# Transformer blocks in one Trainium2 kernel: new orders at the input, in the mixer and in the router, and a memory attention that writes its output by features

## The reference

```python
def causal_depthwise_conv(x, w, b): ...     # width 4, per channel
# hybrid mixer: qk = silu(conv(qk)); the gates i_pre, f_pre are 8 more columns of the same projection

def memory_cross_attention(xn, mn, w_xq, w_xkv, w_xo):
    q = (xn @ w_xq).reshape(B, S, 4, 256)
    k, v = jnp.split(mn @ w_xkv, 2, axis=-1)          # 256 memory rows, 4 heads of 256
    p = softmax(einsum('bshd,bmhd->bhsm', q, k) * 256 ** -0.5)
    return einsum('bhsm,bmhd->bshd', p, v).reshape(B, S, 1024) @ w_xo

# mixture: top group of 4, then top 2 of its 8 experts
g_logits = xt @ w_rg + b_rg;  e_logits = xt @ w_re + b_re
# each token goes to 2 experts; every expert computes (silu(xb @ w1) * (xb @ w3)) @ w2 on blocks of 128 rows
```

## Time and profile before

| | |
|---|---|
| time, median of 3 runs | 2686.95 us (2686.38 to 2688.21) |
| the profiled execution | 2689.78 us, of which its span is 2688.1 us |
| PE busy | 2583.1 us (96%) |
| DVE busy | 1519.3 us (57%) |
| ACT busy | 1238.3 us (46%) |
| POOL busy | 109.4 us (4%) |
| mean granted clock of PE | 0.977 |

### The profile page before, as it was taken

How to read it: one execution, slowest core, us unless ns; L and a number is a source line. 1 busy time by engine, 2 the same in 40 slices (tenths; PEclk the granted TensorE clock), 3 DMA queues, 4 the chain that set the end, 5 groups by cost and what they waited for, 6 DMA issues and landing times.

```text
span 2688.1 us, 30233 instructions
## 1 busy us (share of the span) xinstructions
PE 2583.1 (96%) x12036; PEld 2100.7 (78%) x12036; DVE 1519.3 (57%) x2031; ACT 1238.3 (46%) x1593; POOL 109.4 (4%) x163
## 2 busy tenths in 40 slices
PE   7999999999999999999989999989998999999995
PEld 6767888888787787888867778878877888888884
DVE  5577443343425744434366544354346788888885
ACT  3387322222436732212233333333344787777773
POOL 0111000000230000000000000000001000000001
PEclk9989999999998999999999999999999999999998
DMA  4301234334430033342322032222306999999993
GB/s 142 125 1 32 79 110 133 119 96 139 157 118 1 1 118 110 100 151 94 126 94 94 32 133 93 80 94 77 113 1 268 405 406 406 408 407 406 407 402 143
DMA packets 156901, 431.72 MB, mean 161 GB/s; under 512 B 11067, under 2 KB 80854, under 8 KB 144342
## 3 DMA queue, kind: packets, MB, share of 16 engines
q1 hardware_dynamic: 148726, 400.35, 40.2%
q10 hardware_dynamic: 4736, 16.81, 1.5%
q0 software_dynamic: 3296, 12.58, 1.3%
HBM read 382.53 MB, written 47.19 MB: 160 GB/s over the span
## 4 chain that ended last, share of the span: by engine, by line
PE 88%; DVE 5%; ACT 2%; issue 2%; DMA 1%; POOL 0%; ACTq 0%; POOLq 0%; DVEq 0%
PE ps L314 19%; PE ps L315 19%; PE ps L316 19%; PE ps L2654 6%; PE ps L2652 6%; PE ps L2653 6%; PE ps L996 2%; PE ps L2634 1%; PE ps L1934 1%; PE ps L1641 1%; PE ps L962 1%; PE ps L1614 1%; DVE area L2039 1%; PE ps L2081 1%; PE ps L2681 1%
## 5 line engine op out<-in xcount | busy, mean ns | idle before, releaser
L339 DVE TENSOR_TENSOR area<-area,area 128x2048 fp32r<-128x2048 f32 (+4 forms) x161 | 341.0, 2119 | 573.6 <-ACT area L333 573.6
L316 PE MATMUL ps<-area,area 128*128 128x512 f32 (+2 forms) x1712 | 665.0, 388 | 0.0
L333 ACT ACTIVATE area<-area 128x2048 fp32r<-128x2048 f32 (+4 forms) x161 | 284.5, 1768 | 573.9 <-PE ps L316 567.0
L315 PE MATMUL ps<-area,area 128*128 128x512 f32 (+3 forms) x1368 | 531.2, 388 | 0.0
L2625 DVE TENSOR_TENSOR area<-area,area 128x2048 fp32r<-128x2048 f32 x192 | 433.4, 2286 | 61.6 <-ACT area L2620 61.6
L314 PE MATMUL ps<-actT_parts,area 128*128 128x512 f32 (+1 forms) x984 | 390.1, 396 | 15.1 <-DVE area L339 11.5
L315 PE MATMUL ps<-actT_parts,area 128*128 128x512 f32 (+1 forms) x984 | 388.5, 395 | 0.0
L316 PEld LDWEIGHTS ps<-area,area 128*128 128x128 f32 (+1 forms) x1712 | 321.8, 188 | 71.2
L2620 ACT ACTIVATE area<-area 128x2048 fp32r<-128x2048 f32 x192 | 360.7, 1912 | 18.9 <-PE ps L2654 15.2
L315 PEld LDWEIGHTS ps<-area,area 128*128 128x128 f32 x1368 | 259.8, 190 | 52.7
L314 PE MATMUL ps<-area,area 128*128 128x512 f32 (+2 forms) x728 | 278.8, 383 | 8.3 <-DVE area L737 8.3
(11 more groups left out here) (348 smaller groups left out, 3216.3 us busy)
## 6 DMA issues: line engine op xcount, KB each, us to landing
area<-in_w SPq DMA_DIRECT2D x96, 2048.0 KB, 9.7
area<-in_w_in SPq DMA_DIRECT2D x16, 2048.0 KB, 7.9
area<-in_l_w_gate SPq DMA_DIRECT2D x22, 1024.0 KB, 5.4
area<-in_l_w_up SPq DMA_DIRECT2D x22, 1024.0 KB, 7.9
expert_inputs<-maskz SPq DMA_DIRECT2D x39, 512.0 KB, 8.6
area<-in_l_w_in SPq DMA_DIRECT2D x9, 2048.0 KB, 8.3
expert_rows<-area ACTq DMA_DIRECT2D x32, 512.0 KB, 9.2
area<-expert_inputs SPq DMA_DIRECT2D x31, 512.0 KB, 10.1
```

The costliest lines, as they stand in the source:

```text
L315: pe.matmul(dst(r), a.l, b.h, start=False, stop=False)
L316: m = pe.matmul(dst(r), a.h, b.l, start=False, stop=end)
L333: eng.activation(w.h, raw, ACT.Copy).then_inc(w_hi, 1)
L339: dve.tensor_tensor(w.l, raw, w.high_f, ALU.subtract).then_inc(w_lo, 1)
```

## The change

It has seven parts. (1) x is loaded in four DMAs of 256 features for all tokens, PE turns it chunk by chunk, and ACT copies the odd chunks. (2) In the mixer the second pieces are split ahead of the silu of their tile on ACT, and the first piece of qk2 after the taps of c = 6 instead of c = 7. (3) The memory attention uses the class of the block before it: the exponentials are divided by their sum before the transposes, the values come out by features (4 matmuls of 128x128 a unit instead of 2 of 128x256), and ACT and DVE leave them as high and low parts. Score banks are two instead of three. There is no meeting behind it and no transposing stage. (4) The sums of squares are made ahead of the last chunk of the router's product, the spreading of the root goes, and the logits are scaled after they are turned, four instructions instead of one. (5) The low parts of the first two expert pieces come later on DVE. (6) The rows of expert 0 are made by rows (8 matmuls of 128x512 with `chosen` stationary), copied by ACT and turned like the others. (7) SP loads matrix 6 behind the rows of expert 2.

```diff
+        class WideColumns(Columns):
+            tiles = 2
+            def gathered(self, h):
+                for q in range(2):
+                    yield ps[:, self.vb[h % 2][q], :], self.oT[:, 2 * h + q, :]
+            def peak(self, dve, ch, v, bank, m1):
+                ch(dve.tensor_reduce(m1, bank, AX, ALU.max))
+            def need(self, pe):
+                return lambda k: pe.wait_ge(s_ol, self.ol0 + k + 1)
+            def pe_values(self, pe, u):
...
+                    pe.wait_ge(s_pe, self.pe0 + u + 1)
+                    if i == 0 and h >= 2:
+                        pe.wait_ge(s_ol, self.ol0 + 2 * (h - 1))
...
+                    for q in range(2):
+                        for j in range(nb):
+                            m = pe.matmul(ps[:, self.vb[h % 2][q], i * P:i * P + P], self.pair_values(2 * h + q, j),
+                                          self.PT[:, u % 2, j * P:j * P + P], start=(j == 0), stop=(j == nb - 1))
...
-            gx = Groups(8, "V" * 8)
+            gx = Groups(8, "VA" * 4)
...
-                for t in range(NT):
-                    pe.wait_ge(x_at[t], 16)
-                    for k in range(KD):
...
+                def turn_x(k):
+                    pe.wait_ge(x_at[k // 2], 16)
+                    gx.wait_free(pe, k)
+                    for t in range(NT):
                         m = pe.transpose(ps[:, gx.bank(k), t * P:t * P + P], x_rows[:, t, k * P:k * P + P], ident[:, :])
...
                 for k in range(KD):
+                    if k % 2:
+                        act.wait_ge(tr, trx + k + 1)
+                        act.activation(xT[:, k, :], ps[:, gx.bank(k), :], ACT.Copy).then_inc(ea, 1)
                     norm0.chunk_act(act, k)
...
+                    if c % 4 == 1:
+                        msp.after(act, at_qk[j])
+                    if c == 6:
+                        msp.before(act, 2)
+                    if c == 7:
+                        ij.take_act(act, ifT)
+                        msp.after(act, 2)
                     act.wait_ge(midv, cv0 + c + 1)
                     act.activation(mqk[:, c, :], acc[:, c % 2, :], ACT.Silu,
                                    bias=cols2[:, CB + c:CB + c + 1]).then_inc(mida, 1)
-                    if c % 4 == 1:
-                        msp.after(act, at_qk[j])
-                    if c == 7:
-                        msp.before(act, 2)
-                        ij.take_act(act, ifT)
-                        msp.after(act, 2)
...
+                    if c == 6:
+                        msp.before(dve, 2)
                     if c == 7:
-                        msp.before(dve, 2)
                         msp.after(dve, 2)
...
-            norm, split = out_stage(orow, I["w_xo_2"][0], G_MOE)
+            xat = WideColumns(LH * NT, lambda v: NM, sc_x, None, DH, None, DH ** -0.5,
+                              buffers=(work(to, 4, 512), work(to + 2048, 2, 512)), oT=oT, first=first,
+                              score_banks=(0, 1), turn_banks=(2, 3), value_banks=((4, 5), (6, 7)),
+                              pair_values=lambda g, j: xv[:, j, g * P:g * P + P])
+            stage(lambda pe, ch: xat.pe(pe), lambda act, ch: xat.act(act), xat.dve, None, False)
+            norm, split = product_stage(oT, xat.need, first, I["w_xo_2"][0], G_MOE, row=False)
...
             def first_rows_pe(pe):
...
-                for half in range(2):
-                    for j in range(4):
-                        for t in range(NT):
-                            m = pe.matmul(ps[:, 2 + half, j * P:j * P + P],
-                                          xn[:, t, :].rearrange("p (s k) -> p k s", k=KD)[:, 4 * half + j, :],
-                                          chosen[:, t, :], start=(t == 0), stop=(t == NT - 1))
-                    m.then_inc(m_gt, 1)
+                for c in range(2):
+                    for t in range(NT):
+                        m = pe.matmul(ps[:, 2 + c, :], chosen[:, t, :], xn[:, t, c * 512:c * 512 + 512],
+                                      start=(t == 0), stop=(t == NT - 1))
+                    m.then_inc(m_fr, 1)
+                turn_rows(pe, 0)
+            def first_rows_act(act):
+                for c in range(2):
+                    act.wait_ge(m_fr, c + 1)
+                    act.activation(XR[0][:, c * 512:c * 512 + 512], ps[:, 2 + c, :], ACT.Copy).then_inc(m_fe, 1)
...
                 norm.sums_dve(dve, gt, 1)
-                split_low(dve, 0)
-                norm.wait_row(dve)
                 dve.wait_ge(mm, rw.m0 + 1)
-                dve.tensor_tensor(LT[0:NGR + NE, :], ps[0:NGR + NE, 0, :], rxb[0:NGR + NE, :], ALU.mult).then_inc(m_lt, 1)
+                dve.tensor_copy(LT[0:NGR + NE, :], ps[0:NGR + NE, 0, :]).then_inc(m_lt, 1)
...
-                split_low(dve, 1)
+                split_low(dve, 0)
...
                 dve.tensor_copy(rowu[:, :], rowi).then_inc(m_row, 1)
+                split_low(dve, 1)
...
                     for t in range(NT):
-                        sp.dma_start(x_rows[:, t, :], I["x"][0, t * P:t * P + P, :]).then_inc(x_at[t], 16)
+                        sp.dma_start(x_rows[:, :, 256 * t:256 * t + 256],
+                                     I["x"][0].rearrange("(a p) d -> p a d", p=P)[:, :, 256 * t:256 * t + 256]
+                                     ).then_inc(x_at[t], 16)
...
                 load(5, order[5][0])
-                load(6, order[6][0])
                 sp.wait_ge(m_sc, 16 * 2 * NT)
                 load_rows(1)
                 load(4, order[4][0])
                 load_rows(2)
-                for i in range(7, 3 * NE):
+                for i in range(6, 3 * NE):
```

More of the change, by code:

```diff
@@ L1173, in act @@
                         act.wait_ge(s_o, self.o0 + NT * h + NT)
-                        act.activation(self.oT.h[self.half(h), h // 2, :], self.gathered(h), ACT.Copy).then_inc(s_oh, 1)
+                        for src, d in self.gathered(h):
+                            act.activation(d.h, src, ACT.Copy).then_inc(s_oh, 1)
             def dve(self, dve, ch):
@@ L2359, in sc_x @@
                 return m
-            attention(LH * NT, lambda v: NM, sc_x, lambda u, j: xv[:, j, (u // NT) * DH:(u // NT) * DH + DH], DH,
-                      lambda h, i: orow[:, i, h * DH:h * DH + DH], DH ** -0.5)
-            norm, split = out_stage(orow, I["w_xo_2"][0], G_MOE)
+            first, to = [], 2 * PIECE * (1 - len(pieces) % 2)
+            oT = parts(A0 + 8192, A0 + 12288, KD, S)
+            xat = WideColumns(LH * NT, lambda v: NM, sc_x, None, DH, None, DH ** -0.5,
[4 more added lines that the diff above has]
+            norm, split = product_stage(oT, xat.need, first, I["w_xo_2"][0], G_MOE, row=False)
         if on(7):
@@ L2531, in router_dve @@
                 dve.wait_ge(m_lg, 1)
-                ch(dve.tensor_tensor(LG, ps[:, 1, 0:NT * (NGR + NE)].rearrange("p (t e) -> p t e", t=NT),
-                                     rbias[:, :].rearrange("p (o e) -> p o e", o=1).to_broadcast([P, NT, NGR + NE]),
-                                     ALU.add))
+                norm.wait_col(dve)
+                for t in range(NT):
+                    ch.mark(dve.scalar_tensor_tensor(out=LG[:, t, :],
+                                                     in0=ps[:, 1, t * (NGR + NE):(t + 1) * (NGR + NE)],
+                                                     scalar=rx[:, t:t + 1], in1=rbias[:, :],
+                                                     op0=ALU.mult, op1=ALU.add))
+                ch.wait()
                 G, Ee = LG[:, :, 0:NGR], LG[:, :, NGR:NGR + NE]
```

48 lines of the change are left out of this document (31 added, 17 removed).

## The result

| | before | after | ratio of the runs, 95% interval |
|---|---|---|---|
| median | 2687.78 us | 2665.06 us (2664.27 to 2678.92, 5 runs) | 0.9927 [0.9903, 0.9951] |
| the same pair once more | 2689.86 us | 2665.99 us | 0.9903 [0.9874, 0.9932] |
| PE busy, page | 2583.1 us | 2586.1 us (second profile 2568.3) | |

By the medians the kernel became 22.7 us faster (0.8%); the forecast was 28 (2659, range 2652 to 2669). The sum was 28.5 us; by the spans of two traces, the one before and the second one after, 24.4 us came, so about 4 are missing.

The account below looks back on a forecast made before the run. PE's matmuls were taken as the bound (88% of the span), so gains come from idle time, half clock or removed work: 1.3 + 9.7 + 7.0 + 10.5 = 28.5 us, median forecast 2659 us, range 2652 to 2669.

Parts of the forecast that it names:

- the last term: From the router to expert 1: router, rows and loads together give 10.5 us, ends 6 and 13.5.
- rival (a): Clock falls in the mixer gap, at the attention's start and through expert 0's rows: 20.8 us gained, 2666; chance 0.15.
- Start: Kernel start: first copy of x at 13.87 instead of 15.13, shorter chunk period; 1.3 us, ends 0 and 2.5.
- Mixer: Mixer, ahead of qk2: earlier splitting leaves PE 2.8 us idle instead of 10.02; 9.7 us, ends 7 and 10.7.
- Memory attention: Memory attention to w_xo: transposes, low-part wait and half clock go, two score banks cost some; 7.0 us, ends 4.5 and 7.6.
- Rival (e): Memory attention: units go one after the other, 7.5 us slower in all, 2694.5; decides from 3.7 us a unit; chance 0.03.
- Router: Router: earlier sums and logits turned sooner gain 2.9 us for ranks, `chosen`, positions and the scatter.
- Rows of expert 0: Ahead of expert 0: 16 rows of 512 columns instead of 64 rows; PE starts it 5.8 us earlier, ends 0.6 and 8.2.
- Rows of expert 1: Ahead of expert 1: rows land at 2073, PE wants them at 2074.1, next to no wait; first product 2079.2 instead of 2090.33.
- The rule on the shared ports: Scatter behind the router: DVE's low part holds POOL, making scatter and expert 1's rows 1.3 to 2.3 us later.
- Rival (d): Scatter behind the router: POOL is held by DVE's low part, time 2661; chance 0.10.
- Rival (c): Experts: paced by their loads after all, so the last part gives nothing; 18 us gained, 2669; chance 0.08.

Follow-up runs that it names:

- second execution: The changed kernel run again unaltered, for a base and a second profile: profiled execution 2665.44 us, median 2665.99 us.
- first execution: The first profiled execution of the changed kernel, the slowest of its runs: 2678.92 us, with PE at half clock for 58 us in the first attention.

## Why the prediction was right in its steps but one

The time lies in the range, 6 us above the forecast, and that hides the one miss in part: up to the first product of expert 1 the last term brought 5.6 us less than forecast, and the other three together 2.0 us more. That the time nearly equals rival (a)'s 2666 is luck, as (a) had the loss in the clock at other places. Of the signs that the prediction named one failed: "next to no wait" for the rows of expert 1, where 5.77 us stood.

**Start**, 1.3 forecast, 2.3 measured. The first copy came as worked out. PE's last wait for a low part ended at 23.59 before and at 21.71 in the second execution (the two lines below), and behind it PE had no gap until the sums of squares, where the shift is 2.1 us. The term was mis-sized where I let PE's own 36 matmuls take part of the gain: they took nothing of it. The low parts of the last four chunks come up to 2.4 us earlier, but PE no longer waits for them.

```profile
23.59 0.72 PE L314 MATMUL ps<-area,actT_parts 128*128 128x416 f32 x1 [0.46 <-DVE area L450]
...
21.71 0.72 PE L314 MATMUL ps<-area,actT_parts 128*128 128x416 f32 x1 [0.45 <-DVE area L450]
```

**Mixer**, 9.7 forecast, 10.0 measured, 2.81 us of idle time left for 2.8 forecast. The half clock that I left open came for 3.4 us in the first execution and not in the second, so 8.8 is seen as well; of the eight traces with this idle time of 2.8 us, three show half clock behind it. The order read from the two lists and the durations of the kernel before were enough.

**Memory attention**, 7.0 forecast, 7.7 measured: 6.1 us until the product starts, and 1.6 from the half clock that is gone behind it; none of the ten traces with the new attention shows half clock there, so it is not chance. The first wait cost what was said. Rival (e) needed a unit of 3.7 us; 34.3 us for 16 units exclude it.

**Router**, 2.9 forecast, 3.2 measured. **Rows of expert 0**, 5.8 with the router, 5.8 measured. The granted clock stood at half from about 1.5 us ahead of the first row matmul, and 5.2 to 5.4 us of the matmuls ran at half, where I had 5. Rival (a) had half clock through all of the rows and at the start of the attention; neither came, and the one in the mixer only at times.

**Rows of expert 1.** This step failed: "rows and wish meet within 1 us". PE's wish came as forecast. Before the wait it had worked 17.4 us on expert 0 (17.3). The request for the rows was missed. I had set the scatter, the two matrices and the rows end to end at 406 GB/s: 16.2 us from the first product of expert 0 to the rows. It took 22.7 us in the first execution and 23.2 us in the second. What the runs showed in place of that: the rows can't be asked for before the scatter has landed, and the matrices, issued beside it, share the DMA engines with it, packet for packet, with the larger packets. So the scatter ended behind the matrices, 17.0 us after the first product instead of 14.9 (at 375 GB/s); then 3 us passed nearly idle, and 0.5 MB took 3.8 us from its issue, so the rows came 5.7 us behind instead of 1.3. In the terms of this kernel 4.9 us came out of router, rows and loads together instead of 10.5. The gain of the faster rows of expert 0 brought this on itself: SP waits for the turned rows before it loads matrices 3 and 5. Before, it issued these loads 11.3 us behind POOL's first scatter transfer, when the last had been issued too; now it is 7.3 us, with the last three transfers still to be issued. With matrix 5 behind it the expert parts give 18.2 - 7.7 = 10.5 us up to the turn of expert 1's products (166.33 - 148.16, less the attention). That is the number of the forecast, but in a kernel whose order the forecast didn't have.

**The rule on the shared ports.** The row shows it first: the scatter transfers took 2.23, 2.88 and 1.90 us while DVE made low parts, and 1.24 at most once these were cut short. Each of the three ended 0.8 to 1.0 us behind the low part that ran beside it. The Trainium skill, page "SBUF — State Buffer", section on who interferes with whom, has a two-input DVE operation from SBUF hold up a GpSimd instruction that reads SBUF, and the trace agrees. In the same section it says that a tensor_tensor was not seen to stall a DMA that GpSimd generates; here one did, for 1.0, 1.9 and 0.9 us, so the measurement decides. Rival (d) priced it at 2 us of PE's time; it was 0.6 us of the request. Rival (c) is excluded: of the 24.9 us at expert 1, 24.4 arrived at the end.

## What to carry to other kernels

When a step becomes faster, look up which transfers its end releases and what they will run beside: a bulk load issued into a transfer that someone waits for delays it by its own bytes (4.8 and 6.3 us for 2 MB here). Put the small load that a dependent waits for ahead of bulk loads in time, not only in the queue, and charge a chain of two dependent transfers with the idle hole between them (3 us here). Before moving a load back, look at what stands behind its first consumer on that engine, not only at its last consumer.

## What the runs showed of the hardware that was not expected

A DVE tensor_tensor of 128x2048 with both inputs in SBUF held up a scatter transfer of POOL, which ended 0.8 to 1.0 us behind it (2.23 us in all for the first one, 1.24 when the low parts were cut into four of 128x512). With a scatter and weight loads under way together, the DMA engines moved as many packets of the one as of the other (176 each in 8 us), so the scatter got 0.65 of 3.27 MB. The end of a scatter can trail by a few packets: six in 5 us between the packets of the matrices in the kernel before, where SP waited 1.9 us for them. The same idle time of 2.8 us in the same place was followed by half clock in three of eight traces.
